# Three-branch attention: values as the loaded operand, probabilities weighted before they are turned

## The reference, cut to what matters

```python
# kc, vc: 31 compressed keys and values a group (windows of 32 tokens, two-layer gelu MLP)
s_c = einsum('bqghd,bngd->bghqn', qb, kc) * scale
p_c = masked_softmax(s_c, cmp_end <= t);      o_c = p_c @ vc
# selected blocks (16 of 8: at 512 tokens all of them, so causal attention over all keys)
p_s = masked_softmax(qb @ k_sel * scale, tok_pos <= t);  o_s = p_s @ v_sel
# window of 512 keys: at 512 tokens causal attention too, with keys and values of its own
p_w = masked_softmax(qb @ k_win * scale, valid_w);       o_w = p_w @ v_win
out = gb[..., 0:1] * o_c + gb[..., 1:2] * o_s + gb[..., 2:3] * o_w   # gates per token and head
x = x + out.reshape(b, s, 1024) @ w_out
```

## Time and profile before

| | |
|---|---|
| median of 3 runs | 2272.16 us |
| the profiled execution, its own time | 2273.28 us |
| its span | 2271.4 us |
| TensorE busy | 2047.0 us, 90% |
| VectorE, ScalarE, GpSimd busy | 760.1, 736.1, 547.3 us |
| TensorE in the chain that ended last | 26% of the span as the page gives it |
| last layer's projections, attention, to the output projection | 1505 to 1606, 1621 to 1837, 1851 us |

### The profile page before, as it was taken

One profiled execution on the slowest core, in us unless ns is written; L12 is line 12 of the kernel. 1 busy time (PEld: TensorE's weight loads), 2 busy tenths in 40 slices (PEclk: granted clock), 3 DMA queues, 4 the chain that ended last, 5 costly groups with the idle time before them and its releaser, 6 DMA issues. The chain is left out here.

```text
span 2271.4 us, 27204 instructions
## 1 busy us (share of the span) xinstructions
PE 2047.0 (90%) x10985; PEld 1601.9 (71%) x10985; DVE 760.1 (33%) x1711; ACT 736.1 (32%) x1205; POOL 547.3 (24%) x176
## 2 busy tenths in 40 slices
PE   4999989578775999999999999989899988999998
PEld 3877868422222884566978888879798887888886
DVE  1160352411112326453232222223555633322223
ACT  3223631210112422245332223242454644222232
POOL 1343233000001310000334444423000023444442
PEclk8999999699897997999999999999898989999999
DMA  5323103689996420200223232121020012222220
GB/s 171 111 75 111 38 1 130 253 350 421 421 422 257 155 77 0 74 1 1 75 74 112 75 111 100 71 75 51 25 75 1 1 38 75 77 109 103 83 75 38
DMA packets 82287, 256.24 MB, mean 113 GB/s; under 512 B 10321, under 2 KB 13585, under 8 KB 69873
## 3 DMA queue, kind: packets, MB, share of 16 engines
q1 hardware_dynamic: 70256, 228.14, 26.6%
q0 software_dynamic: 3728, 13.50, 1.7%
q10 hardware_dynamic: 8176, 12.84, 1.5%
HBM read 241.89 MB, written 12.58 MB: 112 GB/s over the span
## 5 line engine op out<-in xcount | busy, mean ns | idle before, releaser
L909 POOL TENSOR_TENSOR w_lo<-ring,w_hi 128x2048 fp32r<-128x2048 f32 (+1 forms) x80 | 366.9, 4588 | 1023.7 <-ACT w_hi L1510 1023.7
L1510 ACT ACTIVATE w_hi<-ring 128x2048 fp32r<-128x2048 f32 (+1 forms) x80 | 151.4, 1892 | 332.2 <-PE psA L1153 332.2
L1948 DVE TENSOR_TENSOR x<-psA,x 128x512 f32<-128x512 f32 (+1 forms) x176 | 108.8, 618 | 330.6 <-PE psA L1153 330.4
L1153 PE MATMUL psA<-hT_hi,w_hi 128*128 128x512 f32 x512 | 201.9, 394 | 9.8 <-DVE hT_lo L1948 9.8
L1153 PE MATMUL psA<-hT_lo,w_hi 128*128 128x512 f32 x512 | 201.5, 393 | 0.0
L1153 PE MATMUL psA<-hT_hi,w_lo 128*128 128x512 f32 x512 | 201.1, 393 | 0.0
L1153 PE MATMUL psA<-w_hi,hid_hi 128*128 128x512 f32 x512 | 199.3, 389 | 0.0
L1153 PE MATMUL psA<-w_hi,hid_lo 128*128 128x512 f32 x512 | 199.2, 389 | 0.0
L1153 PE MATMUL psA<-w_lo,hid_hi 128*128 128x512 f32 x512 | 199.2, 389 | 0.0
L1127 PE MATMUL psO<-big,scr 128*128 128x65 f32 x1120 | 156.1, 271 | 6.1 <-DVE big L1948 5.1
L1153 PE MATMUL psA<-w_hi,hT_hi 128*128 128x256 f32 (+2 forms) x512 | 149.3, 292 | 12.4 <-DVE hT_lo L1948 7.7
(11 more groups left out here) (274 smaller groups left out, 4116.7 us busy)
## 6 DMA issues: line engine op xcount, KB each, us to landing
ring<-in_mlp_w SPq DMA_DIRECT2D x32, 2048.0 KB, 8.2
ring<-in_w_in SPq DMA_DIRECT2D x8, 2048.0 KB, 7.9
ring<-in_w_gate_e SPq DMA_DIRECT2D x14, 1024.0 KB, 12.2
ring<-in_w_up_e SPq DMA_DIRECT2D x14, 1024.0 KB, 14.1
ring<-in_w_down_e SPq DMA_DIRECT2D x13, 1024.0 KB, 14.0
big<-in_w_down_e SPq DMA_DIRECT2D x12, 1024.0 KB, 17.5
ring<-in_ab_w_in SPq DMA_DIRECT2D x5, 2048.0 KB, 8.0
y_dram<-big ACTq DMA_DIRECT2D x16, 512.0 KB, 8.2
```

What stands on the lines that cost most here:

```text
L909: nc.gpsimd.tensor_tensor(part(w_lo, c), raw_piece(c), part(w_hi, c).bitcast(F32), ALU.subtract)\
L1153: ins = pe.matmul(o, a, b, start=(at == 1), stop=(at == 3 * len(terms)))
L1510: return nc.scalar.activation(o, i, f, **kw)
L1948: return nc.vector.tensor_tensor(o, a, b, op)
```

## The change: what it does

1. *Order of items.* One PSUM bank now holds the output of four head pairs for one query tile, over all branches. Its 17 items are 16 pair items (4 heads x 2 branches x 2 groups, the group changing fastest) and one `cmp` item.
2. *Weighting before the turn.* The exponential also sums its row; VectorE takes the reciprocal of the sum; GpSimd multiplies the row of probabilities by the reciprocal and by the gate, in place.
3. *Values as the loaded operand.* 64 columns of values are loaded, the turned probabilities (128 queries) stream. The output is feature-major: group 0 goes to PSUM partitions 0 to 63, group 1 to 64 to 127, one right after the other for each block. All three branches are summed in the bank. The column of ones, the quads' weighting and `add` go.
4. *New lags and buffers.* Turns at i-4, values at i-6 (for both groups at once), 5 buffers of probabilities, 4 of turned ones, still 2 banks `psT`. The copies of turned items are shared: even items on ScalarE, odd ones on VectorE, in iteration i for item i-5, behind the exponential or the mask and the reciprocal.
5. *Compressed scores.* Computed once for all queries with the 32 keys of a group loaded (`compressed_scores`, four jobs), then turned for each `cmp` item.
6. *Compression* moves into the projections: turns after the first half of the first 512 query columns, first layer before the last quarter, second layer after it. The plan of weights follows: `w1k` and `w1v` come before `nq1`.
7. *Output.* Each finished bank becomes a high part (ScalarE) and a low part (VectorE), already feature-major: the eight turns in front of the output projection go. The rows of its weights are loaded in a matching order, by two transfers a piece of 64 partitions each. Its first two pieces are still rounded by ScalarE after its attention loop, and GpSimd subtracts after its last item. The rows of the norm that follows lie in `big` instead of `tok`.

The core of the diff (in order: constants, items, buffers, GpSimd, TensorE, ScalarE, VectorE):

```diff
+TURN_LAG, VALUE_LAG = 4, 6
+PROBS, TURNED = 5, 4
...
+        nsa = []
         for c in range(2):
-            runs = [(g, branch, t) for g in range(2) for branch in range(2) for t in range(NT)]
-            for n, (g, branch, t) in enumerate(runs):
-                pair_group(c, g, branch, t)
-                if n in ((11, 12, 13, 14), (1, 3, 5, 7))[c]:
-                    cmp_group(1 - c, len(cmp_made) % NT)
-        first_cmp = cmp_made[0]
+            for t in range(NT):
+                for j in range(4):
+                    for branch in range(2):
+                        for g in range(2):
+                            nsa.append(dict(kind="pair", c=c, t=t, j=j, branch=branch, g=g, n=(t + 1) * P,
+                                            head=8 * g + 4 * c + j, bank=NT * c + t, first=not branch and not j))
+                nsa.append(dict(kind="cmp", c=c, t=t, g=1, n=2 * P, bank=NT * c + t, index=NT * c + t))
+        n_nsa = len(nsa)
+        last_of = {it["bank"]: i for i, it in enumerate(nsa)}
         n_items = len(items)
+        bank_ending = set(last_of.values())
+
+        def values_before(k):
+
+            return sum(it["g"] for it in nsa[:k + 2 - nsa[k]["g"]])
...
+        probs = [scr[:, i, :] for i in range(5)]
+        turned_probs = [scr[:, 5, :], scr[:, 6, :], a4["probs"][:, 0:T], a4["probs"][:, T:2 * T]]
...
+            for i, it in enumerate(nsa):
+                pool.wait_ge(n_weighed, i + 1)
+                at = probs[i % PROBS][:, 0:it["n"]]
+                if it["kind"] == "cmp":
+                    nc.gpsimd.tensor_tensor(at.rearrange("p (j n) -> p j n", n=32), at.rearrange("p (j n) -> p j n", n=32),
+                                            cmpst[:, it["index"], :].unsqueeze(2).broadcast_to([P, 8, 32]), ALU.mult)\
+                        .then_inc(n_normed, 1)
+                else:
+                    nc.gpsimd.tensor_scalar(at, at, fac[:, n_items + i:n_items + i + 1],
+                                            gate3[:, it["t"], it["head"], 1 + it["branch"]:2 + it["branch"]], ALU.mult, ALU.mult)\
+                        .then_inc(n_normed, 1)
             layer(1, "no")
...
+            def compressed_scores(n):
+
+                o = begin(JOBS["cmps"] + n)
+                for half in range(2):
+                    for g in range(2):
+                        at = 32 * (2 * half + g)
+                        ins = pe.matmul(o[at:at + 32, :], kc[:, 32 * g:32 * g + 32], query(2 * n + half, g).bitcast(F32),
+                                        start=True, stop=True)
+                ins.then_inc(proj_ready, 1)
+
+            def nsa_values(k):
+
+                it, bank_of = nsa[k], nsa[k]["bank"]
+                if k == 0 or nsa[k - 2]["bank"] != bank_of and it["kind"] == "pair":
+                    if bank_of >= 2:
+                        pe.wait_ge(n_out_lo, bank_of - 1)
+                o, pt = psO[bank_of % 2], [turned_probs[(k - 1 + g) % TURNED] for g in range(2)]
+                if it["kind"] == "cmp":
+                    for j in range(4):
+                        for g in range(2):
+                            q = 2 * (j % 2) + g
+                            ins = pe.matmul(o[HD * g:HD * (g + 1), j * P:(j + 1) * P], vcBD[:, HD * q:HD * (q + 1)],
+                                            pt[1][:, j // 2 * P:(j // 2 + 1) * P], start=False, stop=(j == 3))
+                else:
+                    at = it["j"] * P
+                    for b in range(it["t"] + 1):
+                        for g in range(2):
+                            ins = pe.matmul(o[HD * g:HD * (g + 1), at:at + P], v2[:, b, it["branch"], g, 0:HD],
+                                            pt[g][:, b * P:(b + 1) * P], start=(it["first"] and b == 0), stop=False)
+                ins.then_inc(n_values, 1)
+
+            def nsa_attention():
+
+                for i in range(n_nsa + VALUE_LAG):
+                    if 1 <= i <= 4:
+                        queries(i + 3)
+                    elif 6 <= i <= 9:
+                        if i == 6:
+                            copied_all(pe, "turn_nq", 8)
+                            copied_all(pe, "cmpc", 2)
+                        compressed_scores(i - 6)
+                    if i < n_nsa:
+                        it = nsa[i]
+                        if i >= 2:
+                            pe.wait_ge(n_masked, i - 1)
+                        o = psS[i % 2]
+                        if it["kind"] == "cmp":
+                            copied_all(pe, "cmps", 4)
+                            for b in range(2):
+                                ins = pe.transpose(o[:, b * P:(b + 1) * P],
+                                                   cmp_scores[:, 2 * it["c"] + b, it["t"] * P:(it["t"] + 1) * P], ident)
+                        else:
+                            for part in range(2):
+                                ins = pe.matmul(o[:, 0:it["n"]], query(4 * it["c"] + it["j"], it["g"])[:, it["t"] * P:(it["t"] + 1) * P],
+                                                nsa_k[:, it["branch"], it["g"], part, 0:it["n"]], start=(part == 0), stop=(part == 1))
+                        ins.then_inc(n_scores, 1)
+                    k = i - TURN_LAG
+                    if 0 <= k < n_nsa:
+                        pe.wait_ge(n_normed, k + 1)
+                        if k >= 2:
+                            pe.wait_ge(n_copied[k % 2], k // 2)
+                        for b in range(nsa[k]["n"] // P):
+                            ins = pe.transpose(psT[k % 2][:, b * P:(b + 1) * P], probs[k % PROBS][:, b * P:(b + 1) * P], ident)
+                        ins.then_inc(n_turned, 1)
+                    k = i - VALUE_LAG
+                    if 0 <= k < n_nsa and nsa[k]["g"]:
+                        pe.wait_ge(n_copied[k % 2], k // 2 + 1)
+                        if nsa[k]["kind"] == "pair":
+                            pe.wait_ge(n_copied[1 - k % 2], (k + 1) // 2)
+                        nsa_values(k)
...
+            def nsa_attention():
+
+                for i in range(n_nsa + VALUE_LAG + 2):
+                    if 1 <= i <= 4:
+                        queries(i + 3)
+                    elif 6 <= i <= 9:
+                        n = JOBS["cmps"] + i - 6
+                        product(act, n)
+                        A(cmp_scores[:, i - 6, :], bank(n)[:, :], ACT.Copy).then_inc(proj_evacuated[n % 2], 1)
+                    if i < n_nsa:
+                        act.wait_ge(n_masked, i + 1)
+                        at = probs[i % PROBS][:, 0:nsa[i]["n"]]
+                        if nsa[i]["kind"] == "cmp":
+                            A(at, at, ACT.Exp).then_inc(n_probs, 1)
+                        else:
+                            A(at, at, ACT.Exp, bias=negm[:, n_items + i:n_items + i + 1], scale=-1.0,
+                              accum_out=sums[:, n_items + i:n_items + i + 1]).then_inc(n_probs, 1)
+                    k = i - TURN_LAG - 1
+                    if 0 <= k < n_nsa and k % 2 == 0:
+                        act.wait_ge(n_turned, k + 1)
+                        if k >= TURNED:
+                            act.wait_ge(n_values, values_before(k - TURNED))
+                        A(turned_probs[k % TURNED][:, 0:nsa[k]["n"]], psT[k % 2][:, 0:nsa[k]["n"]], ACT.Copy)\
+                            .then_inc(n_copied[k % 2], 1)
+                    k = i - VALUE_LAG - 1
+                    if k in bank_ending:
+                        it = nsa[k]
+                        act.wait_ge(n_values, values_before(k))
+                        A(nsa_out_hi[it["c"]][:, :, it["t"] * P:(it["t"] + 1) * P],
+                          psO[it["bank"] % 2][:, :].rearrange("p (j n) -> p j n", j=4), ACT.Copy).then_inc(n_out_hi, 1)
...
+            def weigh_nsa(k):
+
+                it = nsa[k]
+                dve.wait_ge(n_probs, k + 1)
+                if it["kind"] == "pair":
+                    nc.vector.reciprocal(fac[:, n_items + k:n_items + k + 1], sums[:, n_items + k:n_items + k + 1])\
+                        .then_inc(n_weighed, 1)
+                    return
...
+                    if 1 <= i <= 4:
+                        queries(i + 3)
+                    if i < n_nsa:
+                        it = nsa[i]
+                        dve.wait_ge(n_scores, i + 1)
+                        if i >= PROBS:
+                            dve.wait_ge(n_turned, i - PROBS + 1)
+                        at = probs[i % PROBS][:, 0:it["n"]]
+                        if it["kind"] == "cmp":
+                            s3 = at.rearrange("p (j n) -> p j n", j=8)
+                            st = cmpst[:, it["index"], :]
+                            link(tt(s3, psS[i % 2][:, 0:256].rearrange("p (j n) -> p j n", j=8),
+                                    cmpmask[:, it["t"], :].unsqueeze(1).broadcast_to([P, 8, 32]), ALU.add))
+                            link(nc.vector.tensor_reduce(st, s3, X, ALU.max))
```

(21 more changed lines are left out.)

455 lines of the change are left out of this document (194 added, 261 removed).

## The result

The kernel after takes 2313.01 us (median of 4 runs, 2310.63 to 2314.85); the kernel before, run beside it, 2273.73 us (4 runs, 2270.82 to 2277.34). The ratio is 1.0171, with a 95% interval of 1.0153 to 1.019: slower by 39 us. The forecast was 2309 us. The profiled execution of the changed kernel took 2312.62 us, with a span of 2310.8 us; the span has grown by 39.4 us and the mean granted clock is 0.935, where it was 0.940.

A forecast was written before the change was run, and what follows sets the result against it. TensorE bounds the kernel before; afterwards a loop through the copies of turned tiles does in attention. 36+5+1-7+2 = +37 on 2272.2 gives 2309 us, range 2260 to 2336.

The forecast's parts named there:

- What bounds the kernel: Three-branch attention before the change: TensorE-bound, busy 19.31 of 20 us in a steady stretch, other engines waiting for it.
- Part 1: Value products with values loaded: 0.055 us each, 0.11 for two halves; -23 us if TensorE stayed the bound.
- Part 2: Attention pair loop: turns wait for copies queued behind mask or exponential; 192 us against 156, +36 us.
- P = D + T + V: Pair time: chain from first scores to late turn, plus turns, plus value products; 1.71, 2.83, 3.08, 4.41 us.
- Part 3: Weighting on GpSimd in the attention: between 0.61 and 1.28 us at 512 columns, hidden, cost nothing.
- the port: Rival: GpSimd's weighting also keeps VectorE's masks out, 0.3 us a pair and more; +19, 2328 us; chance 0.05.
- Part 4: Compressed branch in the attention: 23 us before, 28 after with a longer loop, +5 us (-6 if nothing waits).
- the end lag: End of attention: values lag six items instead of three and the last item is compressed; +2 us (0 to 4).
- Part 5: Compression moved into the projections: 17 us before, 18 after, +1 us (-2 to +5).
- Part 6: From last value product into output projection: turns go, 14.3 us becomes 7.1, -7 us (-5 to -9).
- The clock rival: Attention: with TensorE idle a third of the time its granted clock stays at 0.78; +22, 2331 us; chance 0.09.
- TensorE remains the bound: Rival for the attention: copies are early enough, so no loop closes; -33, 2239 us; chance 0.18.

The follow-up runs named there:

- two kernels: ScalarE's rounding of first projection weights moved before last bank copy (two pairs per value visit): 2265.2 us; quartered into late iterations (both copies first): 2244.6 us.
- both copies first: Changed kernel with copies of turned tiles queued ahead of ScalarE's exponential and VectorE's mask: 2251.6 us, ratio 0.9902; repeated, 2252.8 us.

## Why the prediction was right

It said 2309 us by a loop through the copies; 2313 was measured, and the experiments show that loop. That the total fits within 4 us is partly luck, as the point on the sum below says. Step by step:

- **What bounds the kernel.** Right: before, TensorE; after, neither it nor any other engine. The signs that it named are in the profile: turns released by copies, 4.5 us a pair at 512 keys, values 0.055 us apart, GpSimd the releaser four times only (at changes of bank, behind the six operations of a compressed item), 7.2 us in the tail.
- **Part 1, 0.055 us an instruction, 0.11 for two halves.** Right, to the hundredth: 12 starts in 0.66 us. The reason needs a correction: the prediction had the loading of 128 columns set the pace. In one half alone, with 64 columns loaded and 128 streamed, the spacing is 0.11; before, with 128 loaded and 65 streamed, it was 0.105, and a turn, with 128 and 128, also takes 0.11. So loading half as many columns gained nothing by itself; running the halves side by side gained it all. What sets the 0.11 stays open. Switching was taken as 0.15 a visit (bounds 0 and 0.4) and measures 0.22 to 0.32.
- **Part 2, P = D + T + V.** D, from the first scores to the late turn, in the trace: 1.18 us at 128 keys (predicted 1.23), 2.02 at 256 (2.02), 1.91 at 384 (1.94), 2.94 at 512 (2.94). The whole pair: 1.78, 2.95, 3.16 and 4.52 us, against 1.71, 2.83, 3.08 and 4.41. The difference lies in T and V, 0.11 to 0.12 a pair at every width: getting into the half-column shape. In D small errors cancel at 512 keys: from exponential to copy it is 0.72 us where 0.81 was taken (the read of the accumulator overlaps), but from copy to turn 0.72 for 0.65 and from scores to mask 0.77 for 0.74. The sum of 12.41 against 12.03 is worth 6 us over 16 pairs each. The engine whose copy closes the loop is right for the late pairs of a bank at every width, and wrong for its first three pairs, in which the two engines are exchanged.
- **Part 3.** Right: 0.77 us at 512 columns, inside 0.61 to 1.28, hidden. The masks are as long as before (0.69), so the port did nothing to them.
- **Part 4.** A job of compressed scores at the full clock takes 1.07 us where 1.05 was taken, so the four column quarters run side by side (one after the other would be 3.5); two jobs at the lower clock take 1.87. What the compressed items add to the loop was not read.
- **The sum.** Parts 2 and 4 together were +43 with the end lag, and the attention grew by 46.8; the 6 us of the pairs would make it 49. But pairs at these periods make only 199 of the attention's 246 us. The other 47 are compressed items, changes of bank, the start with its queries, and the end. The prediction had 28 + 2 for these. The kernel before has 20 us beyond the 156 + 23 that the prediction counted in it, and if the changed kernel had kept as much, that would make 50. The total fits because what was not counted is about as long on both sides, for which the prediction gave no reason.
- **Part 5.** +1 predicted; by TensorE's starts compression takes 17.6 us in the projections against 16.9 before, where 18 and 17 were taken. **Part 6.** -7 predicted, -7.1 measured, and what was named as late next, ScalarE's copy and rounding and GpSimd's subtraction, was late next; two kernels took it away by about the microseconds that were expected of them.
- **The clock rival.** It is there in part, on both sides. The granted clock was 0.62 from 1780 to 1800 us and averages 0.89 over the attention, 0.93 with both copies first, and 0.94 in the kernel before, which had low stretches of its own (0.78). Pairs read at the full clock already give the predicted loss, and the clock can account for no more than about 15 of the 61 us between the two orders. The rival's working holds a slip: 28% of 1.9 us is 0.53 and not 0.35 us, so that 0.35 can stand only as a mean over the widths.
- **TensorE remains the bound**, 2239 us: what both copies first should then have reached. It stopped at 2252. The waits for copies that are left make 8 us of the 13. Its late pairs take 1.18, 1.70, 2.37 and 3.03 us where 1.03, 1.67, 2.33 and 2.99 were worked out, which makes 4 more: the visits are dearer than Part 1 had, the scores and turns in between cheaper.

## What to carry to other kernels

When a step is moved in an in-order queue, write down the loop that it closes: from the wait at the front of the slowest engine back through every instruction queued ahead of the one that releases it. An engine that is half idle hides nothing if its late operation stands behind one that needs this iteration's input; put work on old data ahead of work on new data. And if such a loop is near its limit, spread the bound engine's long work evenly: fewer, longer visits can cost more than the switches that they save.

## What the runs showed of the hardware that was not expected

- TensorE ran products of two column halves side by side though they were queued one group after the other; up to three on either side of the change of group overlapped, and one group's first started before the other's sixth.
- Loading 64 columns instead of 128 did not shorten the spacing: 0.11 us for value products in one half alone, 0.11 for turns, with 128 columns streamed in both.
- A visit to the half-column shape costs 0.22 to 0.32 us in and out, by two readings of the same trace.
- TensorE's granted clock went to its lower level for 6.8 us behind an idle time of 7.2 us, and stayed at the higher one when the idle time at the same place was 1.5 us.
- GpSimd's multiplication by two factors a partition takes 0.341 us for one column and 0.767 for 512: a fixed third of a microsecond and 0.83 ns a column.
